# Six row buffers and six query tiles held beside the ring in the expert stage of a two-layer transformer kernel

## The chip, the cores and the metric

The kernel runs on one core of one Trainium2 chip. The metric is the time of one execution on the device in microseconds (us). A change under about 0.2% can't be told from none by this measurement.

## What is computed

A batch of one sequence of 256 tokens with width 1024 goes through one block with a mixture of attention and a recurrent mixer, then through a two-layer stack. The change touches the feed-forward part of the first block, a product-key lookup over 16384 experts of one neuron each, in float32:

```python
q = (x @ w_query).reshape(T, 8, 256)                    # 8 heads, two halves of 128
s1, s2 = half scores of q against two sets of 128 sub-keys
v1, i1 = top_k(s1, 16); v2, i2 = top_k(s2, 16)
top_s, top_p = top_k((v1[..., :, None] + v2[..., None, :]).reshape(T, 8, 256), 16)
e_idx = i1[top_p // 16] * 128 + i2[top_p % 16]          # 16 experts a head and token
gate = softmax(top_s)
act = gelu(einsum('cd,ced->ce', x, expert_u[e_idx]))
y = einsum('ce,ced->cd', gate * act, expert_v[e_idx])
```

Each token so reads 128 expert rows; u and v of an expert lie together as one row of 8 KB.

## The kernel before, in words

**Weights.** All weights but the experts come as a stream of tiles of 128 x 1024 float32 (512 KB). A ring of RING = 6 slots holds them; SyncE (SP) refills a slot when its tile has been split (`refill`, L204). A split makes two rounded parts of a tile: ScalarE copies the high part (`high`, L217, the operation on L223), VectorE subtracts it for the low part (`low`, L225, L229) and so frees the slot. Three pairs of parts exist (PAIRS), and two tiles of a stage are split in the stage before it (AHEAD = 2). A product with a tile (`product_both`, L243) is 16 matmuls on TensorE (L247 and L249).

**The expert stage (L1774 to L2232).** T_QUERY = 16 query tiles, two for each of 8 heads. `query(i)` on TensorE makes half a head's query in PSUM, ScalarE copies a part out (`copy_low`, L1970), VectorE adds it up (`out`, L2151). Tiles 0 to 3 are multiplied with x before the norm's shift and scale, and corrected with 16 narrow matmuls each (`constants`, L1851); from tile 4 on the source is the normed h, split anew (L2007 on ScalarE, L2197 on VectorE). `score(h)` multiplies with the sub-keys, `copy_scores(h)` (L1975) puts the scores of both token halves into SBUF. `choose(head)` (L2056) is the top 16 on VectorE, some 30 small operations; there are HEADS = 16 choices, since each of the 8 heads has two halves of 128 tokens (TT = 2). Its last operation (L2115) writes 16 expert numbers a token.

**Rows.** A slot s is one expert for each of 128 tokens; there are 256 slots, 16 to a choice. GpSimd (POOL) issues one indirect DMA a slot (L1839) which gathers 128 rows of 8 KB into buffer s % ROWS, ROWS = 8; it waits until slot s - ROWS has been used on TensorE (`v_used`). VectorE makes the dot product with h_tok (`dot`, L2126, L2131), ScalarE makes gelu (L2023), weight (L2025) and a diagonal matrix (L2030), TensorE adds diag times v to PSUM with two matmuls, four in the records (L1926).

**Order.** Each engine has one in-order program. In the first choice's 16 slots (head 0) the further work is placed by slot numbers written out by hand: `if s == 4: query(6)` on TensorE (L1933 to L1940), the like on ScalarE (L2033 to L2040), and `slot.now in (1, 2, 9, 13)` on VectorE (L2212). `choose(1)` and `choose(2)` run on VectorE within head 0, with a dot at every fourth of their steps (`meanwhile`, L2219); later choices run two heads ahead, with a dot at every second step. Before slot 0, VectorE makes `choose(0)`, the parts of queries 2 and 3, hT (L2192, the normed h) and its low parts (L2197). TensorE transposes hT (`turn_h`, L1887), ScalarE copies it into h_tok (L2010).

Of the kernel before, what the change touches and what calls it, by code (L numbers as in the profile page):

```python
# [22 lines left out]
F32 = mybir.dt.float32  # L23
# [6 lines left out]
P = 128  # L30
# [111 lines left out]
def build(nc, A):  # L142

    with ExitStack() as ctx:
# [68 lines left out]
        def split_no(tile):  # L213

            return tile - T_ADA

        def high(act, tile, turns=0):  # L217

            n = split_no(tile)
            act.wait_ge(loaded[tile % RING], turns * 16 + 16 * (tile // RING + 1))  # L220
            if n >= PAIRS:
                act.wait_ge(tiles_used, turns * RING + (n - PAIRS + 1))
            nc.scalar.activation(wh[:, n % PAIRS, :], ring[:, tile % RING, :], ACT.Copy).then_inc(high_done, 1)  # L223

        def low(dve, tile, turns=0):  # L225

            n = split_no(tile)
            dve.wait_ge(high_done, turns * RING + (n + 1))
            nc.vector.tensor_tensor(wl[:, n % PAIRS, :], ring[:, tile % RING, :],  # L229
                                    wh[:, n % PAIRS, :].bitcast(F32), ALU.subtract).then_inc(tiles_freed, 1)  # L230
# [1520 lines left out]
        def add_gated(col):  # L1751
# [15 lines left out]
                  for free in (mix, sq)]  # L1767
        ROWS = 8
        DIAGS = 4
        HEADS = TT * NH  # L1770
        LOOKAHEAD = 2
        row_in = [sem(f"row_in{i}") for i in range(ROWS)]
        chosen, picked = sem("chosen"), sem("picked")
        with ExitStack() as tmp, stage() as (block, (counted, exp_in, exped, gates_done, dotted, gelued, weighed,  # L1774
# [6 lines left out]
            low_part = sb("query_low", [P, 2, S], where=tmp)  # L1781
            whole = sb("query_whole", [P, 2, S], where=tmp)
            const = sb("query_const", [P, 2], where=tmp)
# [4 lines left out]
            diag = sb("diag", [P, DIAGS, P], where=tmp)  # L1788
            dots, acts, weights = (sb(n, [P, TT * SLOTS], where=tmp) for n in ("dots", "acts", "weights"))
            negmax, den = sb("negmax", [P, HEADS], where=tmp), sb("den", [P, HEADS], where=tmp)  # L1790
# [3 lines left out]
            place, half_at = sb("place", [P, TOPK], U32, where=tmp), sb("half_at", [P, 2, TOPK], U32, where=tmp)  # L1794
            halff, found = sb("halff", [P, 2, TOPK], where=tmp), sb("found", [P, 2, TOPK], where=tmp)
            y_tok = h_tok

# [9 lines left out]
            def score_bank(h):  # L1807
                return ps[:, 6 + h % 2, :]

            def const_columns(i):  # L1810
                return score_bank(min(i, 1))[:, i % 2 * 2:i % 2 * 2 + 2]
# [3 lines left out]
            @block.sync  # L1815
            def _(sp):
                sp.dma_start(subkeys[:, :, :], A["subkeys"]).then_inc(keys_in, 16)
                refill(sp, first, T_QUERY - RING + AHEAD)
                for s in range(TT * SLOTS - ROWS, TT * SLOTS):
                    sp.wait_ge(row_in[s % ROWS], 16 * (s // ROWS + 1))  # L1820
                refill(sp, first + T_QUERY - RING + AHEAD, RING - AHEAD)
# [23 lines left out]
            def _(pe):  # L1845
# [57 lines left out]
                score(0)  # L1903
                query(2)
                query(3)
                score(1)
                turn_h()
                query(4)
                query(5)

# [9 lines left out]
                for s in range(TT * SLOTS):  # L1920
                    t, slot = s // SLOTS, s % SLOTS
                    pe.wait_ge(diag_ready, s + 1)
                    if slot == 0:
                        pe.wait_ge(h_copied, t + 1)
                    for half in range(2):
                        last = nc.tensor.matmul(y_part(t, half), diag[:, s % DIAGS, :],  # L1926
                                                row[:, s % ROWS, D + half * 512:D + (half + 1) * 512],
                                                start=(slot == 0), stop=(slot == SLOTS - 1), skip_group_check=True)
                        if half == 0 and slot == SLOTS - 1:
                            last.then_inc(half_summed, 1)  # L1930
                    last.then_inc(v_used, 1)
                    ahead = ahead_of(s // TOPK)
                    if s == 1:  # L1933
                        score(2)
                    if s == 4:
                        query(6)
                    if s == 8:
                        query(7)
                    if s == 13:
                        score(3)  # L1940
                    if ahead < NH:
                        if s % TOPK == 3:
                            query(2 * ahead)
# [9 lines left out]
            def _(act):  # L1953
# [28 lines left out]
                def weight_and_copy(i):  # L1982
                    high(act, first + AHEAD + i)
                    copy_low(i)
# [27 lines left out]
                weight_and_copy(4)  # L2012
                weight_and_copy(5)
                for s in range(TT * SLOTS):
                    t, slot, head = s // SLOTS, s % SLOTS, s // TOPK
                    if slot % TOPK == 0:
                        if LOOKAHEAD <= head + 1 < HEADS:
                            gate_exp(head + 1)
                        act.wait_ge(gates_done, head + 1)
                    if s == 8:  # L2020
                        gate_exp(1)
# [10 lines left out]
                    ahead = ahead_of(s // TOPK)  # L2032
                    if s == 3:  # L2033
                        copy_scores(2)
                    if s == 7:
                        weight_and_copy(6)
                    if s == 11:
                        weight_and_copy(7)
# [14 lines left out]
            def _(dve):  # L2053
# [94 lines left out]
                def weight(i):  # L2148
                    low(dve, first + AHEAD + i)

# [35 lines left out]
                choose(0, lambda: None)  # L2186
                out(2)
                weight(3)
                out(3)
                for k in range(KT):  # L2190
                    dve.wait_ge(shifted, k + 1)
                    nc.vector.scalar_tensor_tensor(hT[:, k, :], xT[:, k, :], gs[:, 1, k:k + 1], hT[:, k, :],  # L2192
                                                   ALU.mult, ALU.add).then_inc(normed, 1)
                finish_gates(0)
                for k in range(KT):
                    dve.wait_ge(second_high, k + 1)
                    nc.vector.tensor_tensor(srcl[:, k, :], hT[:, k, :], srch[:, k, :].bitcast(F32), ALU.subtract  # L2197
                                            ).then_inc(second_low, 1)
                for head in range(HEADS):
                    slot, calls = counter(), counter()  # L2200

                    def next_dot():
                        dot(head * TOPK + slot.now)
                        slot.one()
                        if slot.now == 6 and LOOKAHEAD <= head + 1 < HEADS:
                            finish_gates(head + 1)
                        if slot.now == 10 and head == 0:
# [769 lines left out]
```

## Time and profile before

| what | us |
|---|---|
| median of 3 runs (2150.57 to 2153.54) | 2150.65 |
| the profiled execution's own time | 2146.91 |
| its span | 2145.1 |
| busy: TensorE, VectorE, ScalarE, GpSimd | 1856.9, 1485.9, 1026.6, 435.1 |
| rows gathered: first issue, last dot | 408.3, 1064.7 |

All times in the text are from the start of the span. The busy shares are means over stages of different kinds: the expert stage lies from 385 to 1072 us, and only it is touched. In 40 equal slices the DMA line of the profile reads 9 or more tenths in slices 9 to 19, with up to 421 GB/s, and 5 or less elsewhere but at the start.

### The profile page before, as it was taken

Reading aid. Unit: us, or ns where it says so; the run is one execution under the profiler, and the core shown is the slowest. Engines: PE = TensorE matmul, PEld = TensorE weight load, DVE = VectorE, ACT = ScalarE, POOL = GpSimd, SP = SyncE. Lnnn points to the kernel's source line nnn. Section 1 sums busy time; section 2 is a strip of 40 time slices with the busy share of each in tenths; the row PEclk is TensorE's granted clock in tenths of the full one; section 3 lists DMA queues with packets and bytes.
Section 4 is the critical chain, followed back from the end, with each engine's and each line's share of the span. In section 5 each row is a group of like instructions: output and inputs, shape, how many; then the busy total and the mean of one; then the engine's idle time right before and its main releaser. Section 6 shows DMA issues by size and latency. Waiting matters only on the chain. (4 is left out here: it accounts for less than half of the span.)

```text
span 2145.1 us, 33417 instructions
## 1 busy us (share of the span) xinstructions
PE 1856.9 (87%) x12148; PEld 1391.5 (65%) x12148; DVE 1485.9 (69%) x2618; ACT 1026.6 (48%) x2065; POOL 435.1 (20%) x457
## 2 busy tenths in 40 slices
PE   4974997898887777787799989889999999779998
PEld 4842887744442222222289988579998988668997
DVE  7676555787776676665466676766677787776666
ACT  2444213554544444444365554467665545435554
POOL 0010220144544344344200000002131330210000
PEclk8987998899999999999999999699999999889999
DMA  9860001599999999999855555035555655224552
GB/s 335 297 228 25 3 3 61 214 416 421 421 421 421 421 421 421 421 420 421 349 170 187 187 192 173 1 128 186 183 179 177 195 177 177 94 96 156 191 186 98
DMA packets 104386, 497.31 MB, mean 232 GB/s; under 512 B 11857, under 2 KB 17233, under 8 KB 71377
## 3 DMA queue, kind: packets, MB, share of 16 engines
q1 hardware_dynamic: 66064, 225.41, 31.4%
q0 software_dynamic: 36864, 268.45, 30.1%
q10 hardware_dynamic: 1344, 1.96, 0.3%
q8 instruction: 69, 1.13, 0.2%
q14 instruction: 45, 0.36, 0.1%
HBM read 494.73 MB, written 1.05 MB: 231 GB/s over the span
## 5 line engine op out<-in xcount | busy, mean ns | idle before, releaser
L247 PE MATMUL ps<-srcs,wh 128*128 128x512 f32 x2064 | 741.7, 401 | 22.7 <-DVE srcs L261 20.4
L1926 PE MATMUL ps<-row,diag 128*128 128x512 f32 x1024 | 498.1, 622 | 114.4 <-ACT diag L2030 114.4
L249 PE MATMUL ps<-srcs,wl 128*128 128x256 f32 x2064 | 582.5, 282 | 0.0
L229 DVE TENSOR_TENSOR wl<-ring,wh 128x1024 fp32r<-128x1024 f32 x362 | 452.3, 1252 | 120.0 <-ACT wh L223 118.8
L247 PEld LDWEIGHTS ps<-srcs,wh 128*128 128x128 f32 x2064 | 392.6, 190 | 114.6 <-issue 27.1
L1926 PEld LDWEIGHTS ps<-row,diag 128*128 128x128 f32 x1024 | 182.9, 193 | 417.4 <-ACT diag L2030 259.0
L2131 DVE CUSTOM_DVE_ANT_0 row<-row,h_tok 128x1024 f32<-128x1024 f32 x256 | 313.5, 1225 | 191.5 <-DMA row<-in_peer_uv,experts 179.2
L223 ACT ACTIVATE wh<-ring 128x1024 fp32r<-128x1024 f32 x362 | 379.2, 1052 | 65.4 <-PE ps L249 43.3
L249 PEld LDWEIGHTS ps<-srcs,wl 128*128 128x128 f32 x2064 | 395.3, 192 | 2.5 <-issue 2.4
L1839 POOL DMA_INDIRECT row<-in_peer_uv,experts x256 | 278.9, 1090 | 385.6 <-PE ps L1926 348.9
L2023 ACT ACTIVATE acts<-dots 128x1 f32<-128x1 f32 x256 | 51.8, 202 | 327.9 <-DVE dots L2131 327.1
L239 PE MATMUL ps<-hidh,wh 128*128 128x256 f32 x704 | 198.9, 283 | 1.9 <-DVE wl L229 1.7
L239 PE MATMUL ps<-hidl,wh 128*128 128x256 f32 x704 | 198.0, 281 | 0.0
L239 PE MATMUL ps<-hidh,wl 128*128 128x256 f32 x704 | 197.3, 280 | 0.0
L239 PEld LDWEIGHTS ps<-hidh,wh 128*128 128x128 f32 x704 | 132.6, 188 | 7.2 <-DVE wl L229 3.6
L239 PEld LDWEIGHTS ps<-hidh,wl 128*128 128x128 f32 x704 | 132.4, 188 | 0.0
L239 PEld LDWEIGHTS ps<-hidl,wh 128*128 128x128 f32 x704 | 132.2, 188 | 0.0
L828 DVE TENSOR_TENSOR gu<-ps,low_part 128x512 f32<-128x512 f32 x88 | 60.7, 690 | 75.8 <-ACT low_part L783 75.8
L783 ACT ACTIVATE low_part<-ps 128x512 f32<-128x512 f32 x88 | 52.6, 598 | 115.1 <-PE ps L249 115.1
L2030 ACT ACTIVATE diag<-mats,weights 128x128 f32<-128x128 f32 x256 | 102.8, 401 | 8.4
L793 ACT ACTIVATE hidh<-hid 128x256 fp32r<-128x256 f32 x88 | 36.8, 419 | 100.6 <-DVE hid L837 94.6
L2462 POOL TENSOR_TENSOR decay<-vecs,dt 128x16 f32<-128x16 f32 x1 | 1.1, 1144 | 385.9 <-ACT dt L2592 385.9
(520 smaller groups left out, 2172.0 us busy)
## 6 DMA issues: line engine op xcount, KB each, us to landing
ring<-in_stream SPq DMA_DIRECT2D x378, 512.0 KB, 3.5
alpha<-in_ada_late SPq DMA_DIRECT2D x12, 512.0 KB, 5.1
beta<-in_ada_late SPq DMA_DIRECT2D x10, 512.0 KB, 5.1
kappa<-in_ada_late SPq DMA_DIRECT2D x10, 512.0 KB, 6.1
row<-in_peer_uv,experts POOLq DMA_INDIRECT x256
bias<-in_attn_bias SPq DMA_DIRECT2D x8, 256.0 KB, 5.7
w<-in_cmp_w SPq DMA_DIRECT2D x1, 2048.0 KB, 7.4
xT<-in_xT SPq DMA_DIRECT2D x1, 1024.0 KB, 15.1
```

Of the source, the lines that this page charges most:

```text
L223: nc.scalar.activation(wh[:, n % PAIRS, :], ring[:, tile % RING, :], ACT.Copy).then_inc(high_done, 1)
L229: nc.vector.tensor_tensor(wl[:, n % PAIRS, :], ring[:, tile % RING, :], wh[:, n % PAIRS, :].bitcast(F32), ALU.subtract).then_inc(tiles_fre ...
L239: last = nc.tensor.matmul(out, left, right, start=(start and p == 0), stop=(stop and p == 2), skip_group_check=True)
L247: nc.tensor.matmul(out, wh[:, n, cols], source.rearrange("p a t -> p (a t)"), start=start, stop=stop, skip_group_check=True)
L249: return nc.tensor.matmul(out[:, 0:S], wl[:, n, cols], source[:, 0, :], start=False, stop=stop, skip_group_check=True)
L783: nc.scalar.activation(low_part[:, j % 2], ps[:, j % 2 * 2:j % 2 * 2 + 2, S:2 * S], ACT.Copy).then_inc(low_copied, 1)
L828: nc.vector.tensor_tensor(gu[:, j % 2], ps[:, j % 2 * 2:j % 2 * 2 + 2, 0:S], low_part[:, j % 2], ALU.add).then_inc(up_ready, 1)
L1839: pool.indirect_dma_start(out=row[:, s % ROWS, :], out_offset=None, in_=A["peer_uv"], in_offset=bass.IndirectOffsetOnAxis(ap=experts[:, t, ...
L1926: last = nc.tensor.matmul(y_part(t, half), diag[:, s % DIAGS, :], row[:, s % ROWS, D + half * 512:D + (half + 1) * 512], start=(slot == 0) ...
L2023: nc.scalar.activation(acts[:, s:s + 1], dots[:, s:s + 1], ACT.Gelu).then_inc(gelued, 1)
L2030: nc.scalar.activation(diag[:, s % DIAGS, :], mat("ident"), ACT.Copy, scale=weights[:, s:s + 1]).then_inc(diag_ready, 1)
L2131: nc.vector.tensor_tensor_reduce(u_row, u_row, h_tok[:, s // SLOTS, :], 1.0, 0.0, ALU.mult, ALU.add, dots[:, s:s + 1]).then_inc(dotted, 1)
```

## The change

- ROWS goes from 8 to 6. The room (16 KB a partition), with that of `whole` (now a view of `hot`) and of `weights` (now `dots` itself), holds `extra`, six tiles. SP loads the last six query tiles (10 to 15) there at the stage's beginning, behind the sub-keys; then four ring tiles (6 to 9), and, as before, the first two tiles of the next stage when query tiles 10 and 11 have been split. For the slots of tiles 10 to 15 SP raises the ring's semaphores itself, so that the numbering stays. `high` and `low` read a held tile from `extra`.
- VectorE: hT is made right behind `choose(0)`, in front of the parts of queries 2 and 3. The second split of h moves from in front of slot 0 to behind dot 2. Dots 0 and 1 stand in front of `choose(1)`. Tiles and queries 4 to 7 move from dots 1, 2, 9, 13 to 6, 8, 12, 14.
- TensorE: `turn_h` moves in front of `query(3)`; queries 4 and 5, which stood in front of slot 0, come behind slots 2 and 4, score(2) behind 6 (1 before), queries 6 and 7 behind 8 and 10 (4 and 8 before).
- ScalarE: exp of choice 0 and the copies of h_tok come in front of `copy_low(3)` and `copy_scores(1)`; the eight copies of the second split come behind slot 1; the rest moves with the queries.

```diff
-        ROWS = 8
+        ROWS = 6
+        EXTRA = RING
@@ sync
                 sp.dma_start(subkeys[:, :, :], A["subkeys"]).then_inc(keys_in, 16)
-                refill(sp, first, T_QUERY - RING + AHEAD)
+                for i in range(EXTRA):
+                    sp.dma_start(extra[:, i, :], A["stream"][first + T_QUERY - EXTRA + i]).then_inc(extra_in[i], 16)
+                refill(sp, first, T_QUERY - EXTRA - RING)
+                for i in range(T_QUERY - EXTRA, T_QUERY):
+                    slot = (first + i) % RING
+                    sp.wait_ge(loaded[slot], 16 * ((first + i) // RING))
+                    sp.sem_inc(loaded[slot], 16)
+                refill(sp, first + T_QUERY - RING, AHEAD)
@@ tensor
                 query(2)
+                turn_h()
                 query(3)
                 score(1)
-                turn_h()
-                query(4)
-                query(5)
...
-                    if s == 1:
+                    if s == 2:
+                        query(4)
+                    if s == 4:
+                        query(5)
+                    if s == 6:
                         score(2)
-                    if s == 4:
+                    if s == 8:
                         query(6)
-                    if s == 8:
+                    if s == 10:
                         query(7)
@@ scalar
-                weight_and_copy(3)
+                high(act, first + AHEAD + 3)
                 gate_exp(0)
-                copy_scores(1)
-                act.wait_ge(tiles_used, split_no(first + UNSHIFTED - 1) + 1)
-                for k in range(KT):
-                    act.wait_ge(normed, k + 1)
-                    nc.scalar.activation(srch[:, k, :], hT[:, k, :], ACT.Copy).then_inc(second_high, 1)
                 for t in range(TT):
                     act.wait_ge(h_turned, t + 1)
                     nc.scalar.activation(h_tok[:, t, :], ps[:, 2 * t:2 * t + 2, :].rearrange("p b n -> p (b n)"),
                                          ACT.Copy, scale=rstd_tok[:, t:t + 1]).then_inc(h_copied, 1)
-                weight_and_copy(4)
-                weight_and_copy(5)
+                copy_low(3)
+                copy_scores(1)
...
+                    if s == 1:
+                        for k in range(KT):
+                            nc.scalar.activation(srch[:, k, :], hT[:, k, :], ACT.Copy).then_inc(second_high, 1)
@@ vector
                 choose(0, lambda: None)
-                out(2)
-                weight(3)
-                out(3)
                 for k in range(KT):
                     dve.wait_ge(shifted, k + 1)
...
+                out(2)
+                weight(3)
                 finish_gates(0)
-                for k in range(KT):
-                    dve.wait_ge(second_high, k + 1)
...
+                out(3)
...
-                        if head == 0 and slot.now in (1, 2, 9, 13):
-                            weight(4 + (1, 2, 9, 13).index(slot.now))
-                            out(4 + (1, 2, 9, 13).index(slot.now))
+                        if head == 0 and slot.now == 3:
+                            split_again()
+                        if head == 0 and slot.now in (6, 8, 12, 14):
+                            weight(4 + (6, 8, 12, 14).index(slot.now))
+                            out(4 + (6, 8, 12, 14).index(slot.now))
...
                     if head == 0:
+                        next_dot()
+                        next_dot()
                         choose(1, meanwhile)
-                        while slot.now < 7:
+                        while slot.now < 9:
```

## Rows read from the trace of the kernel before

**Rows 1.** The page: the software queue's packets, MB, share; the dots' group
```profile
q0 software_dynamic: 36864, 268.45, 30.1%
...
L2131 DVE CUSTOM_DVE_ANT_0 row<-row,h_tok 128x1024 f32<-128x1024 f32 x256 | 313.5, 1225 | 191.5 <-DMA row<-in_peer_uv,experts 179.2
```
**Rows 2.** Windows: length, then busy time and count by engine, PEclk, DMA share, GB/s
```profile
408.30:410.10 1.80, 1.75 (x16) 1.66 (x15) 1.70 (x3) 0.02 (x1) 1.50 (x2) 1.00 0.00 0
...
410.00:420.00 10.00, 7.33 (x31) 6.70 (x31) 8.45 (x24) 7.85 (x17) 7.31 (x7) 0.51 0.98 386
420.00:430.00 10.00, 7.25 (x31) 5.34 (x30) 8.45 (x26) 6.14 (x14) 0.00 (x0) 0.84 1.01 422
```
**Rows 3.** Timeline of POOL: start, us, [idle before <-releaser]; gathers 0 and 8
```profile
408.27 1.17 POOL L1839 DMA_INDIRECT row<-in_peer_uv,experts  x1 [22.43 <-DVE experts L2115]
...
431.51 0.94 POOL L1839 DMA_INDIRECT row<-in_peer_uv,experts  x1 [12.38 <-PE ps L1926]
```
**Rows 4.** Timeline of SP: the stage's twelve ring loads
```profile
386.05 110.69 SPq L208 DMA_DIRECT2D ring<-in_stream  x12
```
**Rows 5.** Timeline of DVE in front of slot 0
```profile
399.81 0.49 DVE L2068 MAX8 top<-mix 128x8 f32<-128x128 f32 x2 [1.18 <-ACT sq L1978]
...
407.80 0.17 DVE L2115 SCALAR_TENSOR_TENSOR experts<-found 128x16 uint32<-128x16 f32 x1
...
411.08 0.48 DVE L2165 SCALAR_TENSOR_TENSOR queries<-rstd,query_const,query_whole 128x256 f32<-128x256 f32 x1
411.48 3.25 DVE L2192 SCALAR_TENSOR_TENSOR hT<-xT,gs,hT 128x256 f32<-128x256 f32 x8
```
**Rows 6.** PE's timeline: score, query 3's narrow matmuls, transposes, slots 2 to 7
```profile
397.64 1.13 PE L1882 MATMUL ps<-subkeys,queries 128*128 128x128 f32 x8 [1.67 <-DVE queries L2165]
...
408.10 0.27 PE L1858 MATMUL ps<-shifts,wh 128*128 128x2 f32 x1 [0.38 <-DVE query_const L2158]
...
414.79 3.67 PE L1891 MATMUL ps<-mats,hT 128*128 128x128 f32 x16 [1.09 <-DVE hT L2192]
...
433.68 5.32 PE L1926 MATMUL ps<-row,diag 128*128 128x512 f32 x12
...
441.67 5.31 PE L1926 MATMUL ps<-row,diag 128*128 128x512 f32 x12
```
**Rows 7.** Timeline of ACT: query 3's copy, a score copy, gelu's table, slot 0's diagonal
```profile
410.08 0.38 ACT L1972 ACTIVATE query_low<-ps 128x256 f32<-128x256 f32 x1 [3.77 <-PE ps L1860]
...
413.73 0.47 ACT L1978 ACTIVATE mix<-ps,rstd_tok 128x256 f32<-128x256 f32 x1 [1.55 <-PE ps L1882]
...
425.52 1.28 ACT L2023 ACT_TABLE_LOAD   x1
...
427.38 0.40 ACT L2030 ACTIVATE diag<-mats,weights 128x128 f32<-128x128 f32 x1
```
**Rows 8.** Timeline of DVE: the second split's low parts, one tile's low part in head 0
```profile
414.99 2.77 DVE L2197 TENSOR_TENSOR srcs<-hT,srcs 128x256 fp32r<-128x256 f32 x8
...
425.10 1.22 DVE L229 TENSOR_TENSOR wl<-ring,wh 128x1024 fp32r<-128x1024 f32 x1
```
**Rows 9.** Timelines of DVE and ACT: dot 16, slot 16's diagonal, dot 23
```profile
463.57 1.22 DVE L2131 CUSTOM_DVE_ANT_0 row<-row,h_tok 128x1024 f32<-128x1024 f32 x1 [2.56 <-ACT sq L1978]
...
467.03 0.40 ACT L2030 ACTIVATE diag<-mats,weights 128x128 f32<-128x128 f32 x1
...
479.39 1.25 DVE L2131 CUSTOM_DVE_ANT_0 row<-row,h_tok 128x1024 f32<-128x1024 f32 x1 [0.31 <-DMA row<-in_peer_uv,experts]
```
**Rows 10.** Timelines in head 3: the issue released by slot 52, and dot 58
```profile
562.91 1.31 POOL L1839 DMA_INDIRECT row<-in_peer_uv,experts  x1 [3.56 <-PE ps L1926]
...
569.64 1.23 DVE L2131 CUSTOM_DVE_ANT_0 row<-row,h_tok 128x1024 f32<-128x1024 f32 x1 [0.76 <-DMA row<-in_peer_uv,experts]
```
**Rows 11.** Windows with PE alone: length, PE busy and count, PEclk, DMA share, GB/s
```profile
410.30:420.40 10.10, 7.68 (x31) 0.50 0.97 393
...
427.40:430.70 3.30, 2.87 (x4) 0.50 1.02 420
```

More of the change, by code:

```diff
@@ L215, in split_no, with high, low @@
             return tile - T_ADA
-        def high(act, tile, turns=0):
+        def high(act, tile, turns=0, held=None):
             n = split_no(tile)
-            act.wait_ge(loaded[tile % RING], turns * 16 + 16 * (tile // RING + 1))
+            source = held[0] if held else ring[:, tile % RING, :]
+            if held:
+                act.wait_ge(held[1], 16)
+            else:
+                act.wait_ge(loaded[tile % RING], turns * 16 + 16 * (tile // RING + 1))
             if n >= PAIRS:
                 act.wait_ge(tiles_used, turns * RING + (n - PAIRS + 1))
-            nc.scalar.activation(wh[:, n % PAIRS, :], ring[:, tile % RING, :], ACT.Copy).then_inc(high_done, 1)
-        def low(dve, tile, turns=0):
+            nc.scalar.activation(wh[:, n % PAIRS, :], source, ACT.Copy).then_inc(high_done, 1)
+        def low(dve, tile, turns=0, held=None):
             n = split_no(tile)
+            source = held[0] if held else ring[:, tile % RING, :]
             dve.wait_ge(high_done, turns * RING + (n + 1))
-            nc.vector.tensor_tensor(wl[:, n % PAIRS, :], ring[:, tile % RING, :],
+            nc.vector.tensor_tensor(wl[:, n % PAIRS, :], source,
                                     wh[:, n % PAIRS, :].bitcast(F32), ALU.subtract).then_inc(tiles_freed, 1)
@@ L1771, in build @@
         LOOKAHEAD = 2
+        EXTRA = RING
         row_in = [sem(f"row_in{i}") for i in range(ROWS)]
+        extra_in = [sem(f"extra_in{i}") for i in range(EXTRA)]
         chosen, picked = sem("chosen"), sem("picked")
@@ L1781, in build @@
             low_part = sb("query_low", [P, 2, S], where=tmp)
-            whole = sb("query_whole", [P, 2, S], where=tmp)
+            extra = sb("extra", [P, EXTRA, D], where=tmp)
             const = sb("query_const", [P, 2], where=tmp)
@@ L1788, in build @@
             diag = sb("diag", [P, DIAGS, P], where=tmp)
-            dots, acts, weights = (sb(n, [P, TT * SLOTS], where=tmp) for n in ("dots", "acts", "weights"))
+            dots, acts = (sb(n, [P, TT * SLOTS], where=tmp) for n in ("dots", "acts"))
+            weights = dots
             negmax, den = sb("negmax", [P, HEADS], where=tmp), sb("den", [P, HEADS], where=tmp)
@@ L1795, in build @@
             halff, found = sb("halff", [P, 2, TOPK], where=tmp), sb("found", [P, 2, TOPK], where=tmp)
+            whole = hot[:, :, :, :].rearrange("p a b c -> p a (b c)")
             y_tok = h_tok
@@ L1808, in score_bank, with extra_at @@
                 return ps[:, 6 + h % 2, :]
+            def extra_at(n):
+                return (extra[:, n, :], extra_in[n]) if 0 <= n < EXTRA else None
             def const_columns(i):
@@ L1982, in weight_and_copy @@
                 def weight_and_copy(i):
-                    high(act, first + AHEAD + i)
+                    n = AHEAD + i - (T_QUERY - EXTRA)
+                    high(act, first + AHEAD + i, held=extra_at(n))
                     copy_low(i)
@@ L2019, in _ @@
                         act.wait_ge(gates_done, head + 1)
-                    if s == 8:
+                    if s == 9:
                         gate_exp(1)
@@ L2032, in _ @@
                     ahead = ahead_of(s // TOPK)
-                    if s == 3:
+                    if s == 1:
+                        for k in range(KT):
+                            nc.scalar.activation(srch[:, k, :], hT[:, k, :], ACT.Copy).then_inc(second_high, 1)
+                    if s == 4:
+                        weight_and_copy(4)
+                    if s == 6:
+                        weight_and_copy(5)
+                    if s == 8:
                         copy_scores(2)
-                    if s == 7:
+                    if s == 10:
                         weight_and_copy(6)
-                    if s == 11:
+                    if s == 12:
                         weight_and_copy(7)
@@ L2148, in weight @@
                 def weight(i):
-                    low(dve, first + AHEAD + i)
+                    n = AHEAD + i - (T_QUERY - EXTRA)
+                    low(dve, first + AHEAD + i, held=extra_at(n))
                 def out(i):
@@ L2193, in _, with split_again @@
                                                    ALU.mult, ALU.add).then_inc(normed, 1)
+                out(2)
+                weight(3)
                 finish_gates(0)
-                for k in range(KT):
-                    dve.wait_ge(second_high, k + 1)
-                    nc.vector.tensor_tensor(srcl[:, k, :], hT[:, k, :], srch[:, k, :].bitcast(F32), ALU.subtract
-                                            ).then_inc(second_low, 1)
+                out(3)
+                def split_again():
+                    for k in range(KT):
+                        dve.wait_ge(second_high, k + 1)
+                        nc.vector.tensor_tensor(srcl[:, k, :], hT[:, k, :], srch[:, k, :].bitcast(F32), ALU.subtract
+                                                ).then_inc(second_low, 1)
                 for head in range(HEADS):
@@ L2206, in next_dot @@
                             finish_gates(head + 1)
-                        if slot.now == 10 and head == 0:
+                        if slot.now == 11 and head == 0:
                             finish_gates(1)
```

## The prediction, made before the changed kernel ran

> **What bounds the kernel now.** The slices of the page say where to look: only in the expert stage do the DMA queues stand at nine tenths or more. The queue row gives 268.45 MB for 256 gathers, 1.049 MB each [rows 1]; at the 422 GB/s of the full window [rows 2] that is 2.49 us a gather, 637 us in all, of the 656 between the first issue and the last dot. The dots' group confirms it: VectorE stood idle 179.2 us until rows had landed [rows 1]. So past the stage's beginning each engine's work is covered by the gathers, and only three things move the end: when the stream starts, holes in it, and other bytes that pass in it. Twelve query and next-stage tiles do [rows 4]; a tile is half a gather, 1.24 us.
>
> The first gather is issued at 408.27 [rows 3], nothing moves until 410.1, then the share is 0.98 and 1.01 [rows 2]: from issue to transfer 1.9 us, and no hole. Eight gathers are 19.9 us; tiles 11 to 13, asked for when splits at 409, 420 and 425 free their slots, add 3.7. That holds until 433.7, and the ninth gather is issued at 431.51, when slot 0 has been used [rows 3].
>
> **Part 1, the tiles.** Tiles 6 to 10 lie before 410 today already; of the seven behind it (11 to 17), five go to the stage's beginning, where eleven loads (5.4 MB, 13 us) have the 24 us between 386 and 410. Gain if the stream has no hole: 5 x 1.24 = 6.2 us. SP's further waits and increments hold up nobody: what is behind them waits for later splits anyway. The first tiles used lie in the ring, so gather 0 does not move, and I take no delay for it.
>
> **Part 2, the beginning.** Six gathers last 14.9 us, until 425. The seventh waits for slot 0. Walked forward:
> - hT right behind the choice: 407.9 + 3.25 [rows 5] = 411.2 (414.7 before).
> - Transposes: 3.67 at the low clock [rows 6], 414.9. TensorE has then stood idle for some 6 us, since query 3 has gone behind them, and in the row at hand it ran at 0.50, 1.2 GHz, between 410.3 and 420.4 [rows 11], behind narrow matmuls and idle time shorter than that. At 2.4 GHz it would be half, 413.1.
> - Query 3: a query is 2.7 to 2.9 us (slots 2 to 4 end at 439.0, slot 5 begins at 441.67 [rows 6]), its narrow matmuls 2.0 (408.10 [rows 6] to the copy at 410.08 [rows 7]). At 2.4 GHz 419.8; with the first part at half clock 420.9.
> - Copy and `out(3)`: from 410.08 [rows 7] to 411.56 [rows 5] is 1.5. So 422.4, and the dots begin here, not at 418.3.
> - Score(1) 1.1 [rows 6], two score copies 0.9, gelu's table 1.28, the three operations to the diagonal's end 1.0 [rows 7]: 426.7. (Exp of choice 0 is earlier than now and lies beside the transposes: nothing.)
> - Slot 0 on TensorE: 2.0 at full clock. At half it took 3.4, and 427.4 to 430.7 was at half now, behind idle time [rows 11]. 428.7 to 430.1; gather 6 is issued 0.3 later and moves 1.9 after that, 431 to 432.3.
>
> The stream so has a hole of 6 to 7 us where none was: the two buffers and 3.7 us of tiles that covered it have both gone. That alone eats the 6.2.
>
> **Part 3, VectorE in head 0.** From 422.4 it has 16 dots (1.15 to 1.22, 19), choices 1 and 2 (8.1 each, from 399.81 to 407.9 [rows 5], 16.2), four splits with their sums (1.22 [rows 8] and 0.3 more, 6), the second split 2.77 [rows 8], gates 0.35: 44.3 us, and 1 to 2 of waiting (for `copy_scores(1)` behind dot 1, for ScalarE's eight copies behind slot 1, 2.5 us). Last dot of the head at 466.7 at least, I take 468.5. Now it ends at 461.0: dot 16 begins at 463.57 after 2.56 idle [rows 9]. The moved split is no extra work, but it stood in a time when VectorE had to wait anyway, and now stands in one when it is the busiest engine. The same holds for queries 4 and 5 on TensorE (5.7 us into head 0); 16 slots are 28 (5.3 for three [rows 6]), with four queries and two scores 41, under VectorE's 44.
>
> **Part 4, where the stream is full again.** Slot 16 is used 8.5 us after the head's last dot: score copies, two table loads, diagonal at 467.43 [rows 9], 2.0 on TensorE, 469.5. None of that is changed: 477.0. With six buffers gather 22 waits for slot 16: issued 477.3, moving 479.2, landed 481.7 and, with some 0.5 for the slowest queue and the semaphore, 482.2; gather 23 at 484.7. In the row of before gather 23 landed at 479.39, dot 23 having waited for it [rows 9]. From here both kernels have the same gathers and the same two tiles to move. Difference: 5.3 us later.
>
> A page gives a price for the landing: the Trainium skill, "DMA: Bandwidth & Descriptors", section "Anatomy of one DMA — SWDGE (gpsimd) path", fits 2.0 us and 436 GB/s for one transfer. By it gather 22 lands 0.5 us earlier and the sum is 4.8.
>
> **Part 5, six buffers later on.** A tight place is gather 58, with a query in front of it: slot 52 is used at 562.6 (its release is the issue at 562.91), so with six it would be issued there, moving at 564.8, landed at about 567.8; it was needed at 569.64, when dot 58 began after waiting for it [rows 10]. Some 2 us remain: nothing. The tail behind the last row is the same.
>
> **Sum.** Between +2 (TensorE at 2.4 GHz throughout: slot 0's end, `out(3)` and with it dot 15 come 3 us sooner) and +6.5 (low clock until 431, landing late). Nearest are the rows of before, half clock where TensorE has just been idle: +5.3, from which I take off 0.7 for VectorE's waits in head 0, which I know only as 1 to 2: +4.6. Against the profiled execution's own 2146.91 this is 2151.5; that execution stood 3.74 under the median of 2150.65, and against the median it is 2155.2.
>
> On the clock the row is the ground: 0.50 behind idle time and narrow matmuls [rows 11]. The Trainium skill, "TensorE: Matmul & The Clock Gate", Part 1, says the same of idle time, half clock after it, full again after sustained work; by it the new idle time in front of the transposes costs what I have put down, and a sum without it would be +2.
>
> **Rivals.**
> - *The hole and the tiles cancel*, 0.27: VectorE's order packs better than I walked it, last dot of head 0 at 465 instead of 468.5. Then +1 or so, 2151.7. For it: my 44.3 is only 1.5 above what VectorE had between 418.3 and 461.0. Against it: the later start of the dots.
> - *Faster*, 0.18: the gain of part 1 comes through. Place: slot 16. If it is used by 471, gather 22 lands by 476.2, where it landed near 476.9 before, and each further us is gained; at 467.5 it is -4 to -5, to the full tiles' 6.2 where no hole opens. 2145.5. The deciding point is the head's last dot: below 462. For it: h_tok comes 3.5 us earlier, ScalarE's two splits no longer precede slot 0 (5.6 us). Against it: query 3, score(1) and its copies now stand in front of slot 0.
> - *Six are too few throughout*, 0.07: if issue to landing under load is 7 us and not 4.9, the 2 us of part 5 are gone in each of heads 1 to 4, two holes of 1 us each: 8 us more, 2163.
> - *The early tiles delay the first ring tiles or gather 0*, 0.03: at most the six loads' 7.5 us. But 13 us of loads have 24, and in front of gather 0 the share is 0.00 [rows 2]; 2 us on top of the forecast, 2157.
> - *My forecast*, 0.45, +2 to +8, 2152.5 to 2158.5.
>
> **How the numbers follow.** 0.2% is 4.3 us, about what a measurement can tell from none. Of my forecast's 0.45 some two thirds lie over it, with the last two rivals slower 0.40; the rest and the cancelling case same 0.42; faster 0.18. The range takes the forecast, the cancelling case and the better half of the spread towards faster: 2148.5 to 2160.
>
> **What would show it.** DMA share well under 1 in 420 to 432 and again around 476 to 479; POOL's seventh issue at 429 to 430.4, where the ninth was at 431.5; first dot at 422.4, dot 15's end near 468.5, dot 23 starting near 484.7 behind DMA; half clock over the transposes. No tile lands between 410 and 480. Behind 485 dots 2.49 us apart as before. Wrong would be a stream without a hole at 425, a head 0 that ends by 463, or waits for rows growing in heads 1 to 4.

## The result and the profile after

The changed kernel took 2160.51 us (median of 6 runs, 2156.57 to 2163.56), the kernel before 2149.35 (6 runs, 2145.66 to 2153.54): ratio 1.0055, 95% interval 1.0045 to 1.0065. It is slower by 11 us; 2155.2 was predicted, and the range ended at 2160.0, so the direction was right and the size was not. The profiled execution took 2162.16, its span is 2160.1, and the stretch from the first gather's issue to the last dot is 666.39 against 656.45. Ahead of the stretch the time is 2.49 us longer, behind it 2.53. I take neither for the change's: the first gather was issued between 407.6 and 412.5 in the kernels below, whatever their edit (the shift lies ahead of the expert stage, as the sub-keys' load shows at the end of this text), and behind the last dot the profiled executions have 1077 to 1083 (after_again, the changed kernel once more, 1080.1 where this one has 1082.9). So the text goes by the stretch, and a time of after is compared with one of before once 2.49 is taken off.

The page of after: DMA share and rate in 40 slices; software queue; dots; issue to landing of the gathers and of the held tiles.

```profile
DMA  8860001689999999999955555035655555224653
GB/s 330 289 234 25 3 3 60 236 335 412 411 409 421 421 418 414 421 417 421 391 185 190 188 182 186 1 117 180 190 181 179 189 180 175 93 89 156 191 188 98
...
q0 software_dynamic: 36864, 268.45, 30.3%
...
L2155 DVE CUSTOM_DVE_ANT_0 row<-row,h_tok 128x1024 f32<-128x1024 f32 x256 | 313.3, 1224 | 193.3 <-DMA row<-in_peer_uv,experts 184.7
...
row<-in_peer_uv,experts POOLq DMA_INDIRECT x256, 10.3
...
extra<-in_stream SPq DMA_DIRECT2D x6, 512.0 KB, 7.4
```

The same bytes pass in the software queue as in [rows 1]; VectorE waits for rows 184.7 us, 5.5 more than before. From slice 9 (counted from 0, 486 us) to slice 11 the rate is 409 to 412 and not 421, though the share reads 9 tenths.

The beginning, timeline of GpSimd: gathers 0, 5 and 6, and gather 22.

```profile
410.76 1.17 POOL L1858 DMA_INDIRECT row<-in_peer_uv,experts  x1 [22.42 <-DVE experts L2139]
...
418.10 0.94 POOL L1858 DMA_INDIRECT row<-in_peer_uv,experts  x1 [0.30 <-issue]
432.94 0.93 POOL L1858 DMA_INDIRECT row<-in_peer_uv,experts  x1 [13.90 <-PE ps L1943]
...
480.15 1.37 POOL L1858 DMA_INDIRECT row<-in_peer_uv,experts  x1 [4.80 <-PE ps L1943]
```

Windows of after with TensorE alone (length, busy and count, PEclk, DMA share, GB/s):

```profile
415.00:417.00 2.00, 2.00 (x12) 0.50 0.92 328
...
419.00:421.00 2.00, 2.00 (x12) 0.84 1.01 414
...
429.00:431.00 2.00, 2.00 (x3) 0.50 0.06 25
431.00:433.00 2.00, 2.00 (x3) 0.50 0.00 0
433.00:435.00 2.00, 2.00 (x5) 0.92 0.30 41
...
479.00:481.00 2.00, 2.00 (x4) 0.50 0.87 369
481.00:483.00 2.00, 2.00 (x6) 0.98 0.53 98
```

The forecast hole stands at 429 to 435: at 421 GB/s the three windows lack (396 + 421 + 380) x 2 / 421 = 5.7 us. In [rows 2] there is none. A smaller one follows at 481, when gather 22 had just been issued. Windows of 50 us with GpSimd alone, first of after, then of before:

```profile
480.00:530.00 50.00, 23.54 (x20) 0.95 0.98 395
530.00:580.00 50.00, 24.34 (x20) 0.97 1.01 416
580.00:630.00 50.00, 22.89 (x19) 0.97 1.00 407
630.00:680.00 50.00, 22.55 (x21) 1.00 1.01 415
```

```profile
480.00:530.00 50.00, 22.89 (x20) 0.97 1.01 420
530.00:580.00 50.00, 26.21 (x20) 0.97 1.01 421
580.00:630.00 50.00, 22.61 (x20) 1.00 1.01 421
630.00:680.00 50.00, 21.64 (x21) 0.97 1.01 421
```

In heads 1 to 4 the share of after hardly falls, and the rate does: between 530 and 680, 5, 14 and 6 of 421 over 50 us each are 3.0 us of transfers. A look at the share alone would miss it.

**The account.** The bytes of all packets between the first issue and the last dot, divided by 421 GB/s, are the time that the stream needs; the rest of the stretch is lost. Lost time by part, in us from the first issue (own sums over the packets of each profiled execution; the last column is the last 20 us, in which the stream runs out). Head 0 is the part up to 72 us, heads 1 to 4 lie in the next two columns, whose end at 272 reaches into head 5:

```
kernel       order buffers held |  MB     need   0-30  30-72 72-122 122-272  to end-20 last 20 | stretch
before       old   8       0    | 272.45  647.1   2.8   0.5   0.1   -0.1    -0.2     6.2     | 656.5
again        old   8       0    | 272.45  647.1   2.8   0.0   0.1    0.0     0.8     6.1     | 656.8
rows7        old   7       0    | 272.45  647.1   4.0   1.4   0.2    0.8     1.7     3.1     | 658.3
rows6        old   6       0    | 272.45  647.1   6.5   3.2   0.3    3.0     2.6     1.9     | 664.6
order8       new   8       0    | 272.47  647.2   3.7   0.9   0.1   -0.1    -0.1     6.0     | 657.7
hold2_old8   old   8       2    | 271.40  644.7   2.7   0.0   0.1   -0.1     0.6     6.3     | 654.2
hold4_old7   old   7       4    | 270.35  642.2   7.5   1.2   0.1    0.0     1.1     4.8     | 656.8
hold6_old    old   6       6    | 269.83  640.9  11.2   2.1   0.6    6.0     1.9     1.8     | 664.5
hold2_new8   new   8       2    | 271.42  644.7   3.8   4.4   1.0   -0.1    -0.1     6.5     | 660.3
after        new   6       6    | 269.84  640.9  10.1   6.8   1.6    2.9     1.9     2.1     | 666.4
after_again  new   6       6    | 269.84  640.9   9.4   6.2   1.3    4.5     2.9     2.5     | 667.7
rows6_short  old   6       0    | 272.43  647.1   7.3   1.0   1.9    0.4     2.5     2.3     | 662.5
after_short  new   6       6    | 269.83  640.9  10.0   6.8   1.9    1.5     4.4     2.1     | 667.6
```

Of after against before: 6.2 us of bytes saved, as predicted; 7.3 + 6.3 lost in head 0, 1.5 + 3.0 from there to 272 us, 2.1 behind, and 4.1 won at the stream's end: +9.9.

### The profile page after: what moved, and what is told of

It reads as the page before. It is cut to its first block and busy times, and to the rows that moved or that the text cites. A ratio compares the mean times of both kernels' runs of the same rounds, so it can differ in the third digit from the quotient of the medians.

```text
span 2160.1 us, 33382 instructions
## 1 busy us (share of the span) xinstructions
PE 1869.2 (87%) x12148; PEld 1399.5 (65%) x12148; DVE 1486.1 (69%) x2618; ACT 1026.0 (47%) x2065; POOL 436.8 (20%) x457
## 5 line engine op out<-in xcount | busy, mean ns | idle before, releaser
L1943 PE MATMUL ps<-row,diag 128*128 128x512 f32 x1024 | 504.9, 629 | 114.0 <-ACT diag L2047 114.0
L234 DVE TENSOR_TENSOR wl<-ring,wh 128x1024 fp32r<-128x1024 f32 x356 | 445.0, 1252 | 119.9 <-ACT wh L227 118.4
L2155 DVE CUSTOM_DVE_ANT_0 row<-row,h_tok 128x1024 f32<-128x1024 f32 x256 | 313.3, 1224 | 193.3 <-DMA row<-in_peer_uv,experts 184.7
L227 ACT ACTIVATE wh<-ring 128x1024 fp32r<-128x1024 f32 x356 | 372.9, 1052 | 67.2 <-PE ps L254 43.4
L2047 ACT ACTIVATE diag<-mats,dots 128x128 f32<-128x128 f32 x256 | 102.8, 401 | 8.3
L2042 ACT ACTIVATE dots<-acts,gates 128x1 f32<-128x1 f32 x256 | 75.4, 294 | 8.3
```

Of the source, the lines that this page charges most:

```text
L227: nc.scalar.activation(wh[:, n % PAIRS, :], source, ACT.Copy).then_inc(high_done, 1)
L234: nc.vector.tensor_tensor(wl[:, n % PAIRS, :], source, wh[:, n % PAIRS, :].bitcast(F32), ALU.subtract).then_inc(tiles_freed, 1)
L2042: nc.scalar.activation(weights[:, s:s + 1], acts[:, s:s + 1], ACT.Copy, scale=gates[:, t, slot:slot + 1]).then_inc(weighed, 1)
L2047: nc.scalar.activation(diag[:, s % DIAGS, :], mat("ident"), ACT.Copy, scale=weights[:, s:s + 1]).then_inc(diag_ready, 1)
L2155: nc.vector.tensor_tensor_reduce(u_row, u_row, h_tok[:, s // SLOTS, :], 1.0, 0.0, ALU.mult, ALU.add, dots[:, s:s + 1]).then_inc(dotted, 1)
```

## The experiments

Each kernel was timed against the kernel before on the same chip, in 6 to 11 runs, but for three that ran once. The yardstick first, the kernel before under another name.

**again**, no edit.

> The kernel before, unchanged, as a yardstick: the stretch from the first gather's issue to the start of the last dot (656.4 us in the profile of before, 666.4 in that of after) should come out within 0.5 us of 656.4, and the ratio at 1.000. If it is off by more than 2 us, differences of that size between two profiles mean nothing.

Measured: ratio 1.0003 [0.9994, 1.0013], 2149.46 us, stretch 656.83. So 0.1% can be told in these comparisons. The two stretches of this kernel lie 0.4 us apart; those of the changed kernel, further down, 1.3.

**rows6**, the buffers alone:

```diff
-        ROWS = 8
+        ROWS = 6
```

> Old order, nothing held, six buffers alone. Theory (the buffers do it: a hole behind gather 5, then holes in heads 1 to 4): the seventh gather waits for slot 0, used at about 431 as before, so a hole of 4 to 6 us, and some 3 us more between gathers 23 and 80 as in the changed kernel; stretch 663 to 667, 0.3 to 0.5% slower. Rival (the new order does it, since VectorE's head 0 ends 7.6 us later): stretch at most 659, within 0.1%.

Measured: 1.0034 [1.0022, 1.0047], 2156.46, stretch 664.62. In the old order, with nothing held, two buffers are worth 8.2 us. Dot 24 is 6.0 us late behind before, dot 80 is 7.7, dot 255 is 8.2. Its windows of GpSimd:

```profile
430.00:480.00 50.00, 22.37 (x18) 0.97 0.94 370
...
530.00:580.00 50.00, 26.39 (x21) 0.97 1.00 412
580.00:630.00 50.00, 23.97 (x20) 1.00 1.00 408
630.00:680.00 50.00, 21.71 (x21) 0.97 1.01 417
```

The low rates at a full share in heads 1 to 4 belong to the six buffers: they are here without the new order and without a held tile.

**order8**, the new order alone: the whole change but for ROWS (8) and the held tiles (all twelve go through the ring).

> New order, eight buffers, nothing held. Theory of the buffers: no hole behind gather 7, gather 24 waits for slot 16 at about 477.4 and lands 1 to 2 us later than before, nothing is lost in heads 1 to 4; stretch 657 to 659. Rival (the order): VectorE's late head 0 costs by itself; stretch 663 or more.

Measured: 1.0015 [1.0005, 1.0026], 2153.21, stretch 657.73, 1.3 us more than before. Dot 15 begins 58.4 us after the first gather (before 51.4), 7.0 late, as the walk of part 3 has it. The stream itself loses only 1.3 us more than before's in head 0, and by dot 28 the dots are back at +1.2. The medians lie 3.7 us apart and not 1.3; one profile a kernel can't say why.

**hold6_old**, buffers and held tiles without the new order:

```diff
-        ROWS = 8
+        ROWS = 6
+        EXTRA = RING
...
+                for i in range(EXTRA):
+                    sp.dma_start(extra[:, i, :], A["stream"][first + T_QUERY - EXTRA + i]).then_inc(extra_in[i], 16)
```

> Old order, six buffers and six held tiles: the change without its new order. If tiles 11 to 15 are worth their 6.2 us even beside a stream with holes, 5 to 6 us shorter than with six buffers alone, stretch 658 to 661; if their transfers had only filled the holes, at most 2 us shorter, 662 to 665. Against the changed kernel's 666.4 the difference is what the new order brings or costs.

Measured: 1.0025 [1.0015, 1.0035], 2154.77, stretch 664.49: the higher of the two bands. By dot 24 the held tiles have brought 2.4 us (lag 3.6 where rows6 has 6.0). By dot 80 the lag is 8.4, and the end is that of rows6. The account says why: they save 6.2 us of bytes, but 4.7 more are lost in the first 30 us, since in rows6 tiles moved while GpSimd waited for slot 0 (two between 15 and 25 us in its packet records, none here), and 3.0 more between 122 and 272:

```profile
530.00:580.00 50.00, 24.82 (x20) 0.97 0.99 399
580.00:630.00 50.00, 22.07 (x20) 0.93 1.00 395
```

**hold2_old8**, old order, eight buffers, and only as many tiles held as fit in the room of `whole` and `weights`:

```diff
+        EXTRA = 2
...
-            whole = sb("query_whole", [P, 2, S], where=tmp)
+            extra = sb("extra", [P, EXTRA, D], where=tmp)
...
-            dots, acts, weights = (sb(n, [P, TT * SLOTS], where=tmp) for n in ("dots", "acts", "weights"))
+            dots, acts = (sb(n, [P, TT * SLOTS], where=tmp) for n in ("dots", "acts"))
+            weights = dots
```

> Old order, eight buffers, and the last two query tiles held from the stage's beginning, in the room of two small buffers that now share others' and what was free. Theory (each tile out of a full stream is worth 1.24 us, and eight buffers keep it full): stretch 2.5 us under the 656.4 to 656.8 of before, 654 to 654.5, ratio 0.999. Rival (the tiles' transfers filled gaps that the stream has anyway): no change, 656 to 657.

Measured: 0.9988 [0.9979, 0.9997], 2146.21 (before 2149.15), stretch 654.23. It is faster than the kernel before by 2.9 us in the medians; the interval, 0.6 to 4.5 us, just leaves out zero. Nothing but the bytes moves in its account: 271.40 MB for 272.45, 2.5 us, of which 2.2 arrive. The stream is full throughout:

```profile
430.00:480.00 50.00, 25.96 (x20) 0.97 1.01 421
...
530.00:580.00 50.00, 23.97 (x20) 0.97 1.01 421
```

**rows7**, the dose between: `ROWS = 7`, nothing else.

> Old order, nothing held, seven buffers. Theory (a buffer's 2.5 us of cover is lost at a time): behind gather 6 a hole of about 2 us, where six buffers have one of about 5; heads 1 to 4 keep 421 GB/s in every 50 us; stretch 658 to 660. Rival (any buffer less weakens the whole stream): GB/s under 420 in heads 1 to 4, stretch 660 or more.

Measured: 1.001 [1.0, 1.0019], 2150.67, stretch 658.33. Eight, seven and six buffers are 656.5, 658.3 and 664.6: the seventh is worth 6.3 us, the eighth 1.8. I had expected 421 GB/s throughout heads 1 to 4; one window has less, 530 to 580:

```profile
530.00:580.00 50.00, 26.53 (x21) 0.97 1.01 413
```

**hold4_old7**, `ROWS = 7` and `EXTRA = 4` in the old order.

> Old order, seven buffers, the last four query tiles held. Theory: in the beginning tiles 11 to 13 still pass (the held ones are 12 to 15, so only 11), the hole behind gather 6 is about 4 us and eats most of the 5.0 us that four tiles are worth; heads 1 to 4 without loss; stretch 656 to 659. Rival (the start sets nothing, heads 1 to 4 set the end): the same 421 GB/s there and stretch 652 to 654.

Measured: 0.9994 [0.9984, 1.0005], 2148.6, stretch 656.77. Four held tiles save 5.0 us of bytes (642.2 for 647.1) and bring 1.6 against rows7: 3.5 go to the first 30 us.

**rows6_short** asks what TensorE's queries do to six buffers. It is rows6, but queries 8 to 15 use one of their eight blocks of the contraction, so that the later part of the scores is not the reference's, and a query lasts 0.4 us on TensorE and not 2.8.

```diff
-                    for k in range(KT):
+                    few = KT if i < 8 else 1
+                    for k in range(few):
```

> Six buffers in the old order, where queries 8 to 15 are made of one of their eight blocks of 128 inputs alone, so that TensorE has 0.4 us instead of 2.8 for each in heads 1 to 4. It leaves out seven eighths of the queries of heads 4 to 7 (the choice of experts there is another one, their number is the same). Theory (in heads 1 to 4 TensorE's queries hold the release of a buffer back until idle queues have to be restarted): 420 GB/s or more in each 50 us from 530 to 680, where six buffers with whole queries had 412, 408 and 417, and a stretch some 2 us shorter, 662.5. Rival (six buffers are too few whatever TensorE does): the same 408 to 417 GB/s and 664.5.

Measured in one run: 2149.14, stretch 662.47. The loss between 122 and 272 us falls from 3.0 to 0.4, but that between 72 and 122 rises from 0.3 to 1.9; together 1.0 us is gained. Of the 2.1 us by which the stretch is shorter, 1.4 stand at dot 15 already (+3.6 for +5.0), ahead of the first short query. So the stretch agrees with the theory's number, but only half of the gain lies where the theory has it. The three windows, the last under the 420 that I had expected:

```profile
530.00:580.00 50.00, 23.78 (x21) 1.00 1.01 423
580.00:630.00 50.00, 23.89 (x20) 1.00 1.01 421
630.00:680.00 50.00, 22.36 (x21) 0.97 1.01 416
```

**after_again**, the changed kernel once more, and **after_short**, the changed kernel with the same short queries (the same part left out).

> The changed kernel, unchanged, as a yardstick for what lies outside the stage's stretch. In its profile the part before the first gather was 2.5 us and the part behind the last dot 2.5 us longer than in the kernel before. If these are chance, they come back to within 1 us or move by themselves (first gather 408 to 413, rest 1079 to 1081), and the stretch stays at 666.4 within 1 us. If they belong to the change, the first gather is at 410.5 or later and the rest at 1082.5 or more again.

> The changed kernel, with queries 8 to 15 made of one of their eight blocks alone, as in the kernel with six buffers before: seven eighths of the queries of heads 4 to 7 are left out. Theory (of the 9.9 us, 6.9 arise in head 0 and some 3 in heads 1 to 4, from TensorE's queries): dot 23 is as late as in the changed kernel, 6.9 us, and no more is lost behind it; stretch 663.0 to 664. Rival (all of it is head 0's, the rest scatter): 666.

Measured in one run each: 2160.5 us with a stretch of 667.66, and 2156.72 with 667.58. The first repeats the result, with its losses placed a little differently (dot 23 at +5.7, dot 128 at +13.3, dot 255 at +11.2). Outside the stretch the rest behind the last dot has gone back, to 1080.1. The first gather has not, at 410.89; but after_short, the same code ahead of the stage, has 408.43. The second missed: I had expected 663 to 664. Its account has the step it was made for, 1.5 between 122 and 272 us for 2.9 and 4.5, and then loses 4.4 behind it, where the other two lose 1.9 and 2.9. Between 72 and 272 us the short queries gain 1.0 us in the old order and 1.1 or 2.4 in the new one, where two profiles of one kernel differ by 1.3. That TensorE's queries are what costs six buffers there is thus likely and not shown, and in the changed kernel the gain does not reach the end; why is not settled.

**hold2_new8**, the new order with eight buffers and two held tiles, is the best version that keeps the new order.

> The new order with eight buffers and two held tiles. If the new order costs by VectorE's late head 0 alone, as with eight buffers and nothing held (657.7 against 656.4), its stretch is 1.3 us over that of the old order with the same buffers and tiles, 655.5; if the held tiles are worth nothing here, because in head 0 the stream waits for VectorE in any case, 657 to 658.

Measured: 1.0016 [1.0006, 1.0026], 2152.57 (before 2149.38), stretch 660.26. Missed as well: not 2.2 us under order8, but 2.5 over it. Windows with TensorE alone, first of order8, then of hold2_new8:

```profile
470.00:480.00 10.00, 6.91 (x16) 1.00 1.02 428
480.00:490.00 10.00, 10.00 (x34) 1.00 1.01 420
```

```profile
470.00:480.00 10.00, 6.91 (x13) 0.89 0.97 396
480.00:490.00 10.00, 10.00 (x32) 0.94 0.83 309
```

In hold2_new8 the granted clock is 0.89 and 0.94 around 480, in TensorE's first slots behind the idle time at the end of head 0, where order8 has 1.00, and slot 16 was used 69.1 us after the first gather, not 67.4. The stream's share falls to 0.83 just there. Its account loses 3.5 us more than order8's between 30 and 72 us and 0.9 more up to 122. That delay, 1.7, fits in, and 2.5 for two tiles: in order8's packet records two tiles move between 45 and 65 us after the first gather, here none. Among the kernels in the new order, order8 and after_again have the full clock at that place and 67.4; after, after_short and hold2_new8 have 69.1 or 69.2. Of the 1.7 us between after_again and after, 1.0 is slot 16 itself at half clock, and 0.7 stood at its start (65.4 and 66.1). The changed kernel itself shows both, so this is no property of a version; with one profile of hold2_new8 I can't say how much of its median it makes.

## Why the prediction missed

**What held.** The bound, and the worth of a tile: 1.24 us, shown by hold2_old8 (2.2 us for two) and by the bytes of after (6.2 us). The walk of head 0, part 2 and part 3, is right to within 0.6 us where it was checked. With 2.49 taken off: transposes from 411.20 to 414.9 (forecast 411.2 and 414.9), first dot 421.89 (422.4), slot 0's diagonal ends at 426.3 (426.7), seventh issue 430.45 (429 to 430.4), the hole 5.7 us and a little at its rims (6 to 7), the head's last dot ends at 468.6 (468.5). VectorE in after, its dots 0, 15, 22 and 23 and the moved split:

```profile
424.38 1.22 DVE L2155 CUSTOM_DVE_ANT_0 row<-row,h_tok 128x1024 f32<-128x1024 f32 x1
...
430.02 2.77 DVE L2224 TENSOR_TENSOR srcs<-hT,srcs 128x256 fp32r<-128x256 f32 x8 [2.10 <-ACT srcs L2052]
...
469.87 1.22 DVE L2155 CUSTOM_DVE_ANT_0 row<-row,h_tok 128x1024 f32<-128x1024 f32 x1
...
486.26 1.23 DVE L2155 CUSTOM_DVE_ANT_0 row<-row,h_tok 128x1024 f32<-128x1024 f32 x1 [1.97 <-DMA row<-in_peer_uv,experts]
...
488.79 1.23 DVE L2155 CUSTOM_DVE_ANT_0 row<-row,h_tok 128x1024 f32<-128x1024 f32 x1 [0.36 <-DMA row<-in_peer_uv,experts]
```

And TensorE, its transposes and slots 0 to 2:

```profile
413.69 3.68 PE L1910 MATMUL ps<-mats,hT 128*128 128x128 f32 x16 [6.28 <-DVE hT L2214]
...
428.88 7.60 PE L1943 MATMUL ps<-row,diag 128*128 128x512 f32 x12 [3.20 <-ACT diag L2047]
```

The clock did what the rows had shown: 0.50 over the transposes and again over slot 0, each behind idle time. The Trainium skill, "TensorE: Matmul & The Clock Gate", Part 1, has half clock behind idle time, and the trace agrees.

**Part 4, the landing, was mis-sized.** Slot 16 and the issue of gather 22 came nearly as predicted (480.15, less 2.49 is 477.66, for 477.3), by some luck: slot 16 began 5.8 us behind the head's last dot where before it was 6.5, and then took 3.0 at half clock, where 2.0 had been put down. From the issue to the landing 4.9 us were put down, and it took 6.1; gathers 0 and 6, also on idle queues, took 5.64 and 5.70. I had read 1.9 from issue to the first bytes and added one full-rate gather; but queues that had run dry do not deliver the first one at the full rate, which a window of the full stream can't show. In the packet records the first 16 packets of gathers 0, 6 and 22 take 0.81, 0.80 and 0.90 us on average, where those of a full stream take 0.31. Gather 23 was used at 488.79, 6.9 us behind the 479.39 of [rows 9] after alignment; 5.3 was the forecast. The 0.7 taken off this for VectorE's waits had no row behind it, and fell with it. Together 2.3 us: 0.4 the later issue, 1.2 the landing, 0.7 the waits. The Trainium skill's price, an estimate from the fit in "DMA: Bandwidth & Descriptors", "Anatomy of one DMA — SWDGE (gpsimd) path", would have been 4.4 us; here 5.6 to 6.1 was measured, and the measurement decides.

**Part 5, "Some 2 us remain: nothing", failed.** The one place that I examined behaved: slot 52 released gather 58 at 573.18, and it landed at 581.46, 2.49 behind gather 57's 578.97. Even there the price was wrong: 8.3 us from issue to landing, with three gathers still ahead of it, for the 4.9 of idle queues. And a landing is that of the slowest of sixteen queues. Windows at the stream's end, GpSimd alone, show how far the queues stand apart; first of before, where the last gather is issued at 1049.47:

```profile
1054.00:1056.00 2.00, 0.00 (x0) 1.00 1.00 418
1056.00:1058.00 2.00, 0.00 (x0) 1.00 0.71 295
1058.00:1060.00 2.00, 0.00 (x0) 1.00 0.29 119
1060.00:1062.00 2.00, 0.00 (x0) 1.00 0.12 49
```

and of after, last issue at 1066.82:

```profile
1072.00:1074.00 2.00, 0.00 (x0) 1.00 0.97 406
1074.00:1076.00 2.00, 0.00 (x0) 1.00 0.44 180
```

By the last packet of each queue, with eight buffers the first six had finished by 1057.6, twelve by 1060, and the slowest at 1064.3, 7 us or nearly three gathers behind the first. With six they end within 3 us. Measured from issue to landing, the median gather has 14.6 us in heads 1 to 4 of hold2_old8 and 9.8 in after; its least is 12.1 there and 7.2 here (530 to 680 us of after). My reading is that a gather's release is needed when the fastest queue is through, and I had checked only against the slowest: the fast queues of six buffers keep running dry and starting again. The packet records bear it out as far as they can without naming an engine. Packets as long as those behind an idle queue (over 0.4 us) stand all along the stream of six buffers, and their time beyond 0.31 us, over sixteen queues, is about what is lost. Between 122 and 272 us it is 3.0 us in after (lost 2.9), 2.4 in rows6 (3.0), 5.0 in hold6_old (6.0) and 0.3 in before (none). Against before, the loss is 4.5 us between 72 and 272, and 2.1 behind; the narrower end gives back 4.1. The third rival, six too few throughout, had the place right, and its condition was met: issue to landing under load is 7.2 us at least, where it asked for 7. Its price, 1 us twice a head, was too high: in the dots' lag behind before it is 3.5 us from dot 24 to dot 80. It had 0.07, and belonged in the sum.

**The first two rivals.** The cancelling one needed head 0 to end by 465, and the faster one by 462; it ended at 468.6. The tiles' 6.2 us were real but spent twice: they would have filled the hole that six buffers open. rows6 against hold6_old shows this without the new order. The last rival, early tiles delaying gather 0, is excluded by SP's timelines, first of before, then of after:

```profile
385.38 0.33 SPq L1817 DMA_DIRECT2D subkeys<-in_subkeys  x1
```

```profile
387.87 0.33 SPq L1829 DMA_DIRECT2D subkeys<-in_subkeys  x1
388.25 4.53 SPq L1831 DMA_DIRECT2D extra<-in_stream  x6
392.82 3.82 SPq L208 DMA_DIRECT2D ring<-in_stream  x4
```

The ring's four loads wait behind the six held tiles, and still the first gather is issued 410.76 - 387.87 = 22.89 us behind the sub-keys' load, as before (408.27 - 385.38). All of the 2.49 us lies ahead of the stage.

**Sum.** Forecast +4.6; +1.6 for gather 22's issue and landing, +0.7 that should not have been taken off, +3.0 net behind dot 23: +9.9, the profiled stretch. By stretches the two buffers make 8 of it (rows6), the new order 1.3 with eight buffers and about 2 with six (after against hold6_old; 3.2 with after_again); the held tiles make nothing with six.

The medians divide it otherwise. Over the kernel before on its own chip, rows6 has 6.9 us, hold6_old 5.2, order8 3.7, and the changed kernel 11.2. The new order with six buffers would be 6 us of it, and the intervals of hold6_old (1.0015 to 1.0035) and of the changed kernel (1.0045 to 1.0065) do not meet. That two buffers cost some 7 or 8 us is so by both; how much the order adds is between 2 and 6 us, and one or two profiles a kernel can't settle it.

**Left open.** How the losses of heads 1 to 4 divide between late releases and slow restarts; what the new order costs with six buffers; why after_short gave back its gain at the end; and what hold2_new8 would measure with the clock of order8 at slot 16. Six-buffer streams end at +8 to +11 whatever their lag was at dot 24 (rows6_short alone at +6.0), and what draws them there I have not shown.

## What to carry to other kernels

Count a buffer of a saturated stream as cover for its fastest queue: price a landing under load from a row under load, check each release against the time when the first queue runs dry, not when the slowest lands, and read the rate beside the share. Bytes taken out of a stream are worth their time only where it stays full; where the buffers' room pays for them, they open the hole that those bytes had filled. Spend the small room that is free (here two tiles, some 3 us faster) and keep the buffers.

## What the hardware showed beyond that

- A gather of 1.049 MB on idle queues landed 5.6 to 6.1 us after its issue, twice its 2.49 us at the full rate; the difference is not only the 1.9 us until the first bytes, since the first packet of a queue that was idle takes 0.8 to 0.9 us on average and not 0.31.
- Share and rate part: 399 and 395 GB/s at a share of 0.99 and 1.00 in hold6_old, where the full stream has 421 at 1.01. In the packet records the 8 KB packets of the gathers usually take 0.31 us; between 480 and 660 us, 10 of before's 9107 take over 0.4 us, and 216 of after's 8800.
- The sixteen queues ended 7 us apart after 650 us of the same work. The Trainium skill, "DMA: Bandwidth & Descriptors", "Latency and other measured facts", has two of the sixteen DMA engines usually slower than the rest. Here the last queue is 7 us behind the first, the next two 5 and 4; that is three late ones, no record here names the engine, and so the trace can neither bear the statement out nor refute it.
- The half clock in head 0 came at different places in two executions of one kernel (after and after_again), and shifted slot 16 by 1.7 us.
